# Head sums of a QK-norm on four column tiles, and its Newton steps over 128 rows

## The reference

```python
qkv = h @ w_qkv
q, k, v = jnp.split(qkv, 3, axis=-1)
q = rms_norm(to_heads(q), q_g)     # over the 64 channels of a head
k = rms_norm(to_heads(k), k_g)
```

## Time and profile before

| | |
|---|---|
| median of three runs | 2128.16 us (2125.97 to 2131.49) |
| profiled execution, time | 2129.64 us |
| profiled execution, span from first to last instruction | 2127.8 us |
| mean granted TensorE clock | 0.985 |
| PE busy | 2057.0 us, 97% of the span |
| DVE busy | 1156.5 us, 54% |
| ACT busy | 689.8 us, 32% |
| POOL busy | 239.9 us, 11% |

### The profile page before, as it was taken

One profiled execution on the slowest core, in us unless ns is written; L12 is line 12 of the kernel. 1 busy time (PEld: TensorE's weight loads), 2 busy tenths in 40 slices (PEclk: granted clock), 3 DMA queues, 4 the chain that ended last, 5 costly groups with the idle time before them and its releaser, 6 DMA issues.

```text
span 2127.8 us, 24505 instructions
## 1 busy us (share of the span) xinstructions
PE 2057.0 (97%) x9576; PEld 1674.8 (79%) x9576; DVE 1156.5 (54%) x1341; ACT 689.8 (32%) x784; POOL 239.9 (11%) x145
## 2 busy tenths in 40 slices
PE   5999999989999999999999999999999999999999
PEld 5888888766577888888788888877878887888887
DVE  7555554587887555533655433364479855333222
ACT  2422322231254332322422322242157644222211
POOL 1100000111211000001100000100025520000000
PEclk9999999999999999999999999999989999999999
DMA  8444543434423444433344322332100022222222
GB/s 322 175 168 187 197 170 124 170 98 135 121 81 119 194 188 170 178 106 107 139 177 178 138 80 96 104 108 78 59 1 1 16 103 79 99 99 81 85 95 94
DMA packets 45415, 261.81 MB, mean 123 GB/s; under 512 B 6416, under 2 KB 7056, under 8 KB 20528
## 3 DMA queue, kind: packets, MB, share of 16 engines
q1 hardware_dynamic: 42288, 256.84, 33.0%
q10 hardware_dynamic: 3072, 4.23, 0.8%
HBM read 250.49 MB, written 2.10 MB: 119 GB/s over the span
## 4 chain that ended last, share of the span: by engine, by line
PE 84%; DVE 7%; issue 3%; DMA 3%; ACT 2%; POOL 1%; SPq 0%; DVEq 0%; POOLq 0%; ACTq 0%
PE ps L1347 26%; PE ps L1349 25%; PE ps L1348 25%; PE ps L1689 2%; DVE w L819 1%; DMA raw<-down_d 1%; PE ps L1368 1%; DMA stage<-ada_d 1%; PE ps L1570 1%; DVE act_tmp L832 1%; DVE ada_acc L832 1%; ACT w L567 1%; PE ps L1608 1%; PE ps L1375 1%; PE ps L1461 1%
## 5 line engine op out<-in xcount | busy, mean ns | idle before, releaser
L1347 PE MATMUL ps<-h_hi,w 128*128 128x512 f32 x1648 | 651.3, 395 | 8.2 <-DVE w L984 6.8
L1349 PE MATMUL ps<-h_hi,w 128*128 128x512 f32 x1648 | 651.0, 395 | 0.0
L1348 PE MATMUL ps<-h_lo,w 128*128 128x512 f32 x1648 | 649.7, 394 | 0.0
L1347 PEld LDWEIGHTS ps<-h_hi,w 128*128 128x128 f32 x1648 | 311.0, 189 | 86.5 <-issue 8.3
L1348 PEld LDWEIGHTS ps<-h_lo,w 128*128 128x128 f32 x1648 | 311.1, 189 | 69.1
L1349 PEld LDWEIGHTS ps<-h_hi,w 128*128 128x128 f32 x1648 | 311.4, 189 | 66.3
L819 DVE TENSOR_TENSOR w<-raw,w 128x1408 fp32r<-128x1408 f32 (+1 forms) x100 | 187.8, 1878 | 210.0 <-ACT w L567 209.9
L567 ACT ACTIVATE w<-raw 128x1408 fp32r<-128x1408 f32 (+1 forms) x100 | 157.0, 1570 | 440.3 <-PE ps L1349 378.2
L1347 PE MATMUL ps<-g_hi,w 128*128 128x512 f32 x704 | 274.8, 390 | 4.2 <-DVE w L819 4.2
L1348 PE MATMUL ps<-g_lo,w 128*128 128x512 f32 x704 | 274.2, 389 | 0.0
L1349 PE MATMUL ps<-g_hi,w 128*128 128x512 f32 x704 | 274.1, 389 | 0.0
(11 more groups left out here) (215 smaller groups left out, 2102.9 us busy)
## 6 DMA issues: line engine op xcount, KB each, us to landing
raw<-up_d SPq DMA_DIRECT2D x88, 1024.0 KB, 6.3
ada_raw<-ada_d SPq DMA_DIRECT2D x64, 1024.0 KB, 4.8
raw<-down_d SPq DMA_DIRECT2D x64, 704.0 KB, 4.1
raw<-mix_d SPq DMA_DIRECT2D x28, 1024.0 KB, 4.8
stage<-ada_d SPq DMA_DIRECT2D x12, 1024.0 KB, 13.2
u_blk<-u SPq DMA_DIRECT2D x64, 64.5 KB, 2.0
u_blk<-u ACTq DMA_DIRECT2D x64, 64.5 KB, 2.1
x<-x_t_d SPq DMA_DIRECT2D x2, 1024.0 KB, 18.2
```

The lines of the kernel that those rows point to most:

```text
L1347: pe.matmul(dst, a_hi_, b_hi_, start=start, stop=False, skip_group_check=True)
L1348: pe.matmul(dst, a_hi_, b_lo_, start=False, stop=False, skip_group_check=True)
L1349: return pe.matmul(dst, a_lo_, b_hi_, start=False, stop=stop, skip_group_check=True)
```

## The change

The head sums are taken for four chunks at once. `head_sums(g)` issues four matmuls, chunk 4g+j on column tile j, so that its sums land in rows 32j to 32j+31 of the bank. It is called after slabs 2, 4, 6 and 8. Two such groups fill a bank, the first starting and the second adding. The factors thus lie over 128 rows, four blocks of 32 of which each holds four heads that count. All steps of `head_factors` and `y_root` work on 128 rows, and `sel` has 128 rows, with its ones in the block in which a chunk's sums lie. Loaded from memory, `sel` is 512 KB instead of 128 KB. The squares of four chunks must be kept until they are summed, so chunks with c mod 4 below 2 go to a new buffer, `sq_qk`, and the others to `sq_tmp`; the square of chunk 4g waits for the group before.

```diff
-            sel = ov("sel", [32, KD, P], F32R)
-            y = ov("y", [32, 4, S])
-            y_hi = ov("y_hi", [32, S], F32R)
-            y_lo = ov("y_lo", [32, S], F32R)
-            sel_f = ov("sel_f", [32, KD, P])
+            sel = ov("sel", [P, KD, P], F32R)
+            y = ov("y", [P, 4, S])
+            y_hi = ov("y_hi", [P, S], F32R)
+            y_lo = ov("y_lo", [P, S], F32R)
+            sel_f = ov("sel_f", [P, KD, P])
...
+            sq_qk = ov("sq_qk", [P, 2, S])
...
+        def qk_square(c):
+            return (sq_tmp if c % 4 >= 2 else sq_qk)[:, c % 2, :]
...
                         act.wait_ge(qk_done, c + 1)
-                        if c == 0:
-                            act.wait_ge(h_done, h_parts(5) + KD // 2)
-                            act.wait_ge(h_odd_done, h_odd_parts(5) + KD // 2)
-                        if c >= 2:
-                            act.wait_ge(ind_done, c - 1)
-                        act.activation(sq_tmp[:, c % 2, :], qk[:, c, :], ACT.Square).then_inc(qksq_done, 1)
+                        if c >= 4:
+                            act.wait_ge(ind_done, c // 4)
+                        act.activation(qk_square(c), qk[:, c, :], ACT.Square).then_inc(qksq_done, 1)
...
-                dve.wait_ge(ind_done, KD * (g + 1))
-                dve.tensor_scalar(y[:, 0, :], ps[0:32, 6 + g, :], 1.0 / HD, EPS, ALU.mult, ALU.add).then_inc(yv_done, 1)
+                dve.wait_ge(ind_done, 2 * (g + 1))
+                dve.tensor_scalar(y[:, 0, :], ps[:, 6 + g, :], 1.0 / HD, EPS, ALU.mult, ALU.add).then_inc(yv_done, 1)
...
-            def head_sums(c):
+            def head_sums(g):
                 pe.wait_ge(con_s, 48)
-                pe.wait_ge(qksq_done, c + 1)
-                pe.matmul(ps[0:32, 6 + c // KD, :], ind[:, c % KD, :], sq_tmp[:, c % 2, :], start=(c % KD == 0),
-                          stop=(c % KD == KD - 1)).then_inc(ind_done, 1)
+                pe.wait_ge(qksq_done, 4 * g + 4)
+                for j in range(4):
+                    last = pe.matmul(ps[32 * j:32 * j + 32, 6 + g // 2, :], ind[:, (4 * g + j) % KD, :],
+                                     qk_square(j), start=(g % 2 == 0), stop=(g % 2 == 1), skip_group_check=True)
+                last.then_inc(ind_done, 1)
...
-                if 1 <= s <= 8:
-                    head_sums(2 * s - 2)
-                    head_sums(2 * s - 1)
+                if s in (2, 4, 6, 8):
+                    head_sums(s // 2 - 1)
...
-    sel = np.zeros((32, KD, P))
+    sel = np.zeros((P, KD, P))
...
-            sel[2 * c + b, c, HD * b:HD * (b + 1)] = 1.0
+            sel[32 * (c % 4) + 2 * c + b, c, HD * b:HD * (b + 1)] = 1.0
```

## The result

| | before | after |
|---|---|---|
| median | 2125.64 us (six runs) | 2114.75 us (six runs) |
| ratio | | 0.9949, interval 0.9933 to 0.9964 |
| profiled execution, time | 2129.64 us | 2117.56 us |
| profiled execution, span | 2127.8 us | 2115.8 us |

The change is faster by 0.51%, some 11 us; 9.75 were forecast. But the median of before stands at 2125.64 over six runs, not at the 2128.16 of three from which the forecast was counted, and 2114.75 lies 0.75 us under the range. So the direction and the size were right and the absolute time was not. Two things had to be found out: whether the 9.75 us came about in the places that were named, and where the rest of the difference between the two profiles, 12.0 us of span, is from. Three single executions at a much lower granted clock, of 2296.70, 2923.39 and 3191.78 us, are left out of every mean, median and ratio here.

A forecast was written before the change was run, and what follows sets the result against it. TensorE, busy 97% of the span, was taken as the bound; savings summed slab by slab to 9.75 us, taking the median from 2128.16 to 2118.4 us. The range for all was 2115.5 to 2123.5 us.

The forecast's parts named there:

- slab 1: No burst after this slab, but TensorE then waits for VectorE's next low half: 0.40 us saved instead of 2.04.
- slab 2: Burst after this slab becomes four sums on four column tiles, 1.32 us in place of 2.16: 0.84 saved.
- slab 3: The burst of two head sums after this slab is removed whole: 2.04 us saved.
- slabs 4 and 5: First spread waits for VectorE's factors, limiting the gain to 2.49 us, plus 0.20 at the spread's exit: 2.69.
- slab 6: Shorter burst of head sums saves 0.84 us and the spread's exit 0.20: 1.04.
- slab 7: Removed burst saves 1.92 us, the 128-row spread 0.11 on entry and 0.20 on exit: 2.23.
- Two waves: Each new group's eight passes on four column tiles overlap, starting in two sets 0.43 us apart; burst 1.32 us, not 2.16.
- Rival 2: Tiles do not overlap in short groups; eight passes run serially, 3.88 us for 2.16: 2126.3 us, no change; chance 0.07.
- Where VectorE ends last: After slabs 1, 4, 8 and 11 TensorE waits for VectorE, so savings there are cut or lost.
- Work put at nothing: 128-row square roots, multiplications, casts and reciprocal, sel's 512 KB load and the squares' own buffer were taken to cost nothing.
- Rival 1, the clock: TensorE's new wait after slab 1 brings a stretch at half clock, at most 1.7 us lost: 2120.1 us; chance 0.14.
- so the median goes to 2118.4: Last step: the 9.75 us saving was taken off the before kernel's median of 2128.16 us.

The follow-up runs named there:

- e_one_tile: Changed kernel with its four groups of head sums all on one column tile, factors and selector on 32 rows; median 2121.20 us, ratio 0.9990 to before.
- e_pairs: Kernel before's order, two sums after each slab, but each pair on two of four column tiles, factors and selector over 128 rows; 2114.63 us, ratio 0.9954.
- e_casts_late: Changed kernel with VectorE's casts of con and sel moved behind its work for slab 1; median 2109.79 us, ratio 0.9934 to before.
- e_mid: Changed kernel with the second and fourth group of sums taken inside slabs 4 and 8 and factors made right behind; 2110.65 us, ratio 0.9933 to before.
- e_spread32: Changed kernel with each spread taking only the 32-row block holding its chunk's sums, not all 128 rows; median 2113.43 us, ratio 0.9945 to before.

## Why the prediction was right or wrong

**Step by step, the sum held.** Saved, by the distances of slabs from the end of slab 1 to each slab's second matmul: slab 1 0.40 (forecast 0.40); slab 2 0.84 (0.84); slab 3 2.05 (2.04); slabs 4 and 5 2.61 (2.69); slab 6 1.04 (1.04); slab 7 2.2 (2.23), when 0.2 of slow spacing in before is taken off. To the first matmul of `logits` it is 9.87 against the profiles of before without the halved stretch (forecast 9.75). That the whole agrees to 0.1 us is in small part luck: the slow spacing, of which the sum had nothing, gave 0.6 us and took 0.4.

**Two waves.** Right, and shown from both sides: e_one_tile, where overlap is taken away, keeps 0.65 us of 10.08; e_pairs shows that two tiles cost as much as four. Rival 2 is out.

**Where VectorE ends last.** Right, and shown by e_casts_late and e_mid: take the wait away and its time comes back. At slab 5, 0.08 us less was saved than reckoned: seven VectorE steps of the factors each took 0.01 to 0.02 us more on 128 rows.

**Work put at nothing.** Right. The load of sel, 512 KB, landed in 4.8 us and was read 19 us after its issue.

**Rival 1, the clock.** It did not come after slab 1 in any of three profiles of the changed kernel. Whether a halved stretch follows a wait is open: in the first profile of before one followed a wait of 0.77 us behind slab 9, in the other two the same wait was followed by none.

**The step that failed** is the last, "so the median goes to 2118.4". The term that was off is the starting point, not the saving: 2128.16 was the median of three runs, and 78 runs of before have a mean of 2125.0. From that 9.75 gives 2115.3, inside 2113.95 to 2117.56, the runs of after. I had "a median of a few by about 1.5" for the scatter and put the range's lower end only 2.9 under the forecast. Runs of one kernel differ by up to 13 us (2118.48 to 2131.49), and the traces show from what: halved stretches of the clock and 200 us at a time with a spacing of 0.233 in place of 0.229. Neither was in the range. To a lesser part the saving was short as well: with 10.4 us between the means, some 0.6 are outside the sum. The slow spacing in the last block, 4.2 us where it comes, was in two of three profiles of before and in none of the changed kernel's, and would give this much and more; that the change itself makes it rarer there is not shown, three profiles each are too few.

**Open.** What turns the spacing to 0.233 and back, and why the form of the spreads decides it in slabs 9 and 11. The attention, from last spread to the first matmul with the output weights, took 148.9, 147.0 and 148.9 us in before's profiles and 152.4, 149.5 and 147.0 in after's, with halved clock for 27.3 us on end in the longest. If the change gave something back there, three profiles do not show it, since the last has none of it.

## What to carry to other kernels

Here a burst of small float32 matmuls cost an entry, a number of waves and an exit; sums on two more column tiles cost nothing, and a burst left out saved all of its price where no other engine was late. Before the saving of a removed interruption is booked, follow the other engines' chains that start from the same event: of the eight bursts, slab 1's paid 0.40 of 2.04 us, slab 8's nothing, and slabs 4 and 5 lost 0.3, until the casts and the factors were moved, and moving them was worth a third of the change again. Count a forecast as a ratio to many runs, and check a few microseconds on a distance inside the trace, with the spacing within it looked at. Let that distance end behind the next wait: ended ahead of it, the stage credited e_spread32 with 2.0 us where 0.9 were kept.

## What the runs showed of the hardware that I had not expected

Two spreads with 32 rows each, on different groups of 32 partitions, run at once (e_spread32, both at 1467.94), without any change to how they are issued: high and low of one spread, then high and low of the next. The second spread's high matmul starts 0.34 us before the first one's low matmul, which stands ahead of it in the program. The spacing of 128x512 matmuls has two values at full granted clock, 0.229 and 0.233 us, and holds the slower one for up to 220 us (859 against 875 matmuls in 200 us). For 256 columns they are 0.113 and 0.118 us, and which of them slabs 9 and 11 have went with the rows of the spreads in all 14 profiles. The cast of `con` took 1.42 us beside a subtraction on GpSimd and 0.42 in its later place without one; that GpSimd is the cause was not tested. Which rows the factors take, 32 or 128, made 0.01 to 0.02 us for each instruction on VectorE.
